# Two modulation groups moved into the loop over the first two units, their loads ahead of the residual's spill, and the reads of the gate tile shared by two engines

## What is computed

```python
mod = (jax.nn.silu(c) @ w_ada + b_ada)[:, None, :]
sh1, sc1, gt1, sh2, sc2, gt2 = jnp.split(mod, 6, axis=-1)
h = rmsnorm(x, g_mix) * (1 + sc1) + sh1
z = h @ w_in
u, q, k, v, o, ig, fg, gp, gm = jnp.split(z, IN_SPLITS, axis=-1)
# a pooling mixer on u, an mLSTM on q, k, v, ig, fg, merge gates gp, gm, then
x = x + gt1 * (merged @ w_out)
# and an FFN with its own modulation sh2, sc2, gt2, and a last norm
```

## Time and profile before

| | us |
|---|---|
| median of 3 executions | 1986.21 (1984.85 to 1988.93) |
| the profiled execution | 1987.68 |
| its span, first to last instruction | 1985.5 |
| PE busy | 1912.7 (96%) |
| DVE, ACT, POOL busy | 698.3, 450.1, 103.6 |
| mean granted clock of PE | 0.983 of 2.4 GHz |

### The profile page before, as it was taken

One profiled execution on the slowest core, in us unless ns is written; L12 is line 12 of the kernel. 1 busy time (PEld: TensorE's weight loads), 2 busy tenths in 40 slices (PEclk: granted clock), 3 DMA queues, 4 the chain that ended last, 5 costly groups with the idle time before them and its releaser, 6 DMA issues.

```text
span 1985.5 us, 28627 instructions
## 1 busy us (share of the span) xinstructions
PE 1912.7 (96%) x11797; PEld 1847.4 (93%) x11797; DVE 698.3 (35%) x1240; ACT 450.1 (23%) x708; POOL 103.6 (5%) x217
## 2 busy tenths in 40 slices
PE   7999999999999999887899999999999999999997
PEld 5899999999999999766799999999999999999997
DVE  5311110013333333343735482343343244244236
ACT  5321211123333333412202122111111111111113
POOL 0010047010000000021000000000000000000000
PEclk9999999999999999988899999999999999999999
DMA  9653345342333333587743401111111111111102
GB/s 338 224 166 127 122 138 158 120 140 70 103 102 102 102 102 102 152 223 248 254 147 101 142 12 64 43 43 42 42 42 53 42 42 42 42 42 50 45 32 90
DMA packets 219344, 211.12 MB, mean 106 GB/s; under 512 B 13499, under 2 KB 187439, under 8 KB 219279
## 3 DMA queue, kind: packets, MB, share of 16 engines
q1 hardware_dynamic: 210093, 176.29, 29.1%
q10 hardware_dynamic: 7786, 29.57, 3.7%
q0 software_dynamic: 1408, 4.46, 0.7%
HBM read 156.00 MB, written 54.41 MB: 106 GB/s over the span
## 4 chain that ended last, share of the span: by engine, by line
PE 90%; DMA 4%; DVE 3%; ACT 1%; SPq 1%; issue 1%; ACTq 0%; DVEq 0%
PE dense L1867 79%; PE misc L2116 1%; PE misc L2120 1%; DMA z_scratch<-stage 1%; PE dense L2293 1%; PE misc L1956 1%; PE misc L2089 1%; DMA out_dram<-cst 1%; PE misc L2118 1%; PE dense L1924 1%; DMA out_dram<-cs 1%; SPq L587 1%; PE misc L2227 0%; PE dense L2016 0%; PE misc L2097 0%
## 5 line engine op out<-in xcount | busy, mean ns | idle before, releaser
L1867 PE MATMUL dense<-act_hi,w_hi 128*128 128x384 f32 (+1 forms) x2616 | 615.8, 342 | 11.8 <-DVE act_lo L1288 6.8
L1867 PE MATMUL dense<-act_hi,w_lo 128*128 128x384 f32 (+1 forms) x2616 | 583.1, 329 | 0.0
L1867 PE MATMUL dense<-act_lo,w_hi 128*128 128x384 f32 (+1 forms) x2616 | 583.0, 329 | 0.0
L1867 PEld LDWEIGHTS dense<-act_hi,w_hi 128*128 128x128 f32 x2616 | 451.8, 189 | 28.8 <-issue 15.6
L1867 PEld LDWEIGHTS dense<-act_hi,w_lo 128*128 128x128 f32 x2616 | 450.0, 189 | 3.0 <-issue 3.0
L1867 PEld LDWEIGHTS dense<-act_lo,w_hi 128*128 128x128 f32 x2616 | 448.9, 189 | 1.3 <-issue 1.3
L1273 DVE TENSOR_TENSOR w_lo<-raw,w_hi 128x1024 fp32r<-128x1024 f32 x131 | 160.9, 1229 | 508.7 <-ACT w_hi L857 508.6
L857 ACT ACTIVATE w_hi<-raw 128x1024 fp32r<-128x1024 f32 x132 | 139.8, 1059 | 298.3 <-PE dense L1867 287.4
L1867 PE MATMUL dense<-a_hi,w_lo 128*128 128x384 f32 (+1 forms) x480 | 106.3, 329 | 0.0
L1803 DVE SCALAR_TENSOR_TENSOR hmT<-dense,mod,hmT 128x768 f32<-128x768 f32 x80 | 81.4, 1017 | 69.3 <-PE dense L1867 68.8
L1867 PE MATMUL dense<-a_lo,w_hi 128*128 128x384 f32 (+1 forms) x480 | 105.7, 328 | 0.0
(11 more groups left out here) (316 smaller groups left out, 1519.5 us busy)
## 6 DMA issues: line engine op xcount, KB each, us to landing
z_scratch<-stage ACTq DMA_DIRECT2D x52, 544.0 KB, 2.7
raw<-in_w_in_dram SPq DMA_DIRECT2D x53, 512.0 KB, 3.6
raw<-in_w_gate_up_dram SPq DMA_DIRECT2D x44, 512.0 KB, 3.6
ada_w<-in_w_ada_dram SPq DMA_DIRECT2D x20, 1024.0 KB, 7.0
stage<-z_scratch SPq DMA_DIRECT2D x24, 544.0 KB, 3.8
raw<-in_w_down_dram SPq DMA_DIRECT2D x22, 512.0 KB, 3.5
oin<-z_scratch SPq DMA_DIRECT2D x16, 544.0 KB, 4.4
qkv<-z_scratch SPq DMA_DIRECT2D x8, 1024.0 KB, 6.0
```

The lines of the kernel that those rows point to most:

```text
L1867: ins = pe.matmul(tile(k, c), w[:, off:off + P], x[:, xr, t0:t1], start=(first and p == 0), stop=(last and p == 2))
```

## The change

On SP, ada loads 8 and 9 go ahead of the spill of xT; 10 and 11 stay behind it. On PE, groups 8 and 9 are computed inside the loop: product 8 at the end of step kk = 4, turn 8 in step 5, product 9 at the end of step 5, turn 9 in step 6. ACT reads their rows and mods between the high parts of the last four row blocks. Once the gate tile is full, ACT makes the high split of weight tile 2 first and then reads only the gate rows of partitions 0 to 7; DVE copies those of partitions 32 to 39 and then makes the low split.

```diff
@@ SP
             for j in range(2):
                 load(2 + j, w_cols(w_in[0], P * (1 + j)))
+            for a in range(KT, ADA0 // 2):
+                ada_load(a)
 
             for s in range(2):
                 sp.wait_ge(tile_free[s], T_SS // 2)
             sp.dma_start(z[Z_X:Z_X + KT].rearrange("k p t -> p k t"), xT[:, :, :]).then_inc(x_spilled, 16)
 
-            for a in range(KT, ADA0 // 2 + 2):
+            for a in range(ADA0 // 2, ADA0 // 2 + 2):
                 ada_load(a)
@@ ACT
             for p in range(1, KT // 2):
-                if p < KT // 2 - 1:
-                    h_high(2 * p)
-                    group_mod(2 * p + 2)
-                    h_high(2 * p + 1)
-                    group_rows(2 * p + 3)
-                    group_mod(2 * p + 3)
-                    if 2 * p + 4 < KT:
-                        group_rows(2 * p + 4)
-                else:
-                    h_high(2 * p)
-                    h_high(2 * p + 1)
-            for a in range(KT, ADA0 // 2):
-                ada_out(a)
+                h_high(2 * p)
+                group_mod(2 * p + 2)
+                h_high(2 * p + 1)
+                group_rows(2 * p + 3)
+                group_mod(2 * p + 3)
+                if 2 * p + 4 < ADA0 // 2:
+                    group_rows(2 * p + 4)
             act.wait_ge(rest_in, rest)
 
             wait_full(act, tile_full, T_GATE)
+            split_hi(2)
             s = 3 * (T_GATE % 2)
-            for a in range(2):
-                kw_ = {"bias": gbias[:, 0:1]} if a == 0 else {}
-                rows, p0 = gates[32 * a:32 * a + 8, :], 32 * a
-                act.activation(wide(rows), dense[p0:p0 + 8, s:s + 2, 0:384], ACT.Copy if a else ACT.Identity, **kw_
-                               ).then_inc(gates_ready, 1)
-                act.activation(rows[:, 768:T], dense[p0:p0 + 8, s + 2, 0:320], ACT.Copy if a else ACT.Identity, **kw_
-                               ).then_inc(gates_ready, 1)
+            act.activation(wide(gates[0:8, :]), dense[0:8, s:s + 2, 0:384], ACT.Identity, bias=gbias[:, 0:1]
+                           ).then_inc(gates_ready, 1)
+            act.activation(gates[0:8, 768:T], dense[0:8, s + 2, 0:320], ACT.Identity, bias=gbias[:, 0:1]
+                           ).then_inc(gates_ready, 1)
             act.wait_ge(gates_ready, 4)
             act.sem_inc(tile_free[T_GATE % 2], 1)
-            split_hi(2)
@@ DVE
             for p in range(KT // 2):
                 first_rows(p)
+            wait_full(dve, tile_full, T_GATE)
+            s = 3 * (T_GATE % 2)
+            dve.tensor_copy(wide(gates[32:40, :]), dense[32:40, s:s + 2, 0:384]).then_inc(gates_ready, 1)
+            dve.tensor_copy(gates[32:40, 768:T], dense[32:40, s + 2, 0:320]).then_inc(gates_ready, 1)
             split_lo(2)
@@ PE
                     one_pass(T_L1, 1, P * kk, kk, p, kk == 0, end, act_hi, act_lo)
-                    if p == 0 and kk + 3 < KT:
+                    if p == 0 and kk + 3 < ADA0 // 2:
                         group_turn(kk + 3)
                 one_pass(T_L1, 1, P * kk, kk, 2, kk == 0, end, act_hi, act_lo)
-                if kk + 4 < KT:
+                if kk + 4 < ADA0 // 2:
                     group_product(kk + 4)
-            for a in range(KT, ADA0 // 2):
-                group_product(a)
-                group_turn(a)
```

## The result

The changed kernel took 1989.03 us at the median of 20 executions (1987.22 to 1995.16), the kernel before 1986.05 on the same chip (20 executions, 1982.23 to 1990.20). The ratio is 1.0016, 95% interval 1.0009 to 1.0022: slower by 1.8 to 4.4 us.

The account below looks back on a forecast made before the run. The prediction took L1867's dense matmuls as the bound, losing time in the gap ahead of unit 2 and at half clock. A start 0.5 us later less 0.25 gave about +0.3, median 1986.5 us, range 1983.0 to 1990.2.

Parts of the forecast that it names:

- What bounds the stage: Between loop and unit 2: a 9.7 us gap, then half clock costing unit 2 1.95 us; at most about 11.7 us.
- Part 1: Groups 8 and 9 inside the loop: products at 61.4 and 65.5 without waits, adding 3.24 us; 4.9 leave the gap.
- Part 2: Split first, gate reads shared by ACT and DVE: low split done at 73.8, unit 2 could start at 73.9.
- Part 3: Spill behind load 9 on SP: load 10 lands at 77.4, unit 2 starts at 79.1, 0.5 us later than before.
- The half clock: In unit 2: 3.4 us lie at half clock instead of 3.9, which gives 0.25 us back.
- The sum: Whole kernel: +0.5 for unit 2's start less 0.25 of half clock, about +0.3 us, median 1986.5.
- B: Ahead of unit 2: load 10 isn't held back, landing before 72.9; unit 2 at 73.9, full clock, 1979.6 us; chance 0.15.
- C: Idle ahead of group 10's product: clock doesn't fall, product takes 1.00, unit 2 at 78.5; -2.1 us, 1984.1; chance 0.10.
- D: Ahead of unit 2: load 10 at 80.6 beside ACT's store, unit 2 at 82.3, longer half clock; +5.1, 1991.3; chance 0.07.

Follow-up runs that it names:

- the first pair: First traces of the unchanged kernel before and of the changed kernel; unit 2 ends 1.6 us later in the changed one.
- the second: Second traces of the same two kernels, nothing altered in either; unit 2 ends 2.2 us later in the changed one.

## Why the prediction was right, and where its number was off

- **What bounds the stage.** Right: the gap ahead of unit 2 and the clock behind it. Both were to be had: unit 2 ends at 88.3 with the old order of loads and at 87.2 with load 10 ahead as well, against 92.6 before, all of it at full clock.
- **Part 1.** Right to the tenth: products at 61.75 and 65.89 (61.4 and 65.5, the whole start 0.4 us later), no wait, ACT's late row block unnoticed. The remark that loads 8 and 9 as slow as before (7.5 and 6.2) would cost 0.3 us was sound for the wait, 0.53 us with a load 8 of 7.65; but the load can take 9.0, and then it was 1.92 and 1.6 more at half clock.
- **Part 2.** Right: copies of 0.95 and 0.47 (0.96 and 0.4), low split done at 74.2 (73.8 and the 0.4 of the start).
- **Part 3.** Right in mechanism: the spill ahead of load 10 in one queue, a wait on ada_w, half clock behind it. The sizes: load 10 at 79.1 and not 77.4, made of the start (0.4), load 9's flight (6.3, not 5.4), the spill (11.1, not 10.7). The product took 1.94, not the 1.66 of a trace in which part of it ran at full clock. So unit 2 at 81.1 instead of 79.1. That load 10 left at 62.93, where I had 62.6, was luck: I held it back by 3.71 us for the spill's issue, which took 0.53, and what held it was its ring buffer, given back as group 8's rows were read at 62.9. The half clock gave 0.86 back in the first pair, 0.7 in the second, where I had 0.25: unit 2 started later than I had it, and lay in the stretch at half clock for 2.1 us (81.1 to 83.2) instead of 4.0 (78.6 to 82.6).
- **The sum.** +0.3 forecast; +1.6 and +2.2 at the end of unit 2 in the two pairs, +3.2 (1.8 to 4.4) at the medians. The mis-sized term is the landing of load 10, 1.3 us without the shift of the start. The 1.5 us near 275 stood in no term. That the median lies in the range owes something to its width, which holds the scatter of single executions.
- **The rivals.** B needed load 10 by 72.9: it took another order of issue. C fell, the clock was 0.59 at the mean from 75.8 to 79.1 and the product took 1.94. D had a landing of 80.6; load 10 landed midway between that and the forecast's 77.4, and +3.2 is nearer to D's +5.1 than to +0.3. The condition given for D, a landing later than 77.0, did not part it from the forecast, whose own landing is later too. D's reason failed: ACT's store, issued at 75.22, took 6.3 us instead of 2.8, but no packet of it moved before 79.1, when load 10 had landed, so it cost load 10 nothing. And where two queues do meet, the engines were not halved between them: the shares went by rows, so long rows beside a load would have taken four fifths.

The Trainium skill (DMA: Bandwidth & Descriptors, "Queues, rings and completion order") has the descriptors of a ring consumed in ring order: the landings of the changed kernel agree, 11.1 and 3.0 us apart. It also has the DMA engines change between queues at packet granularity: the pair with load 10 in ACT's queue agrees, 16.6 us beside long rows and 10.2 beside short ones, with 696 rows to 698 and 926 to 925. Whether the engines change after every row or after a run of rows, these counts don't tell.

## What to carry to other kernels

When loads are moved ahead of a large store, ask which transfer now stands first behind it, and when its consumer comes in the engine's order: here the two loads that were moved had 1.9 and 0.8 us to spare, and the third, left behind, held up all that followed for 6.6. One line further, with load 10 ahead as well, the change gave 4 to 9 us. Most of that is the work in the loop and the shared reads: with the loads left behind the spill it gave 3.6 to 8.4. Another queue was no way past a store with long rows, since the two queues' shares went by rows and not by bytes. And compare where the stage ends, not only where it starts: a later start met less half clock and gave part of the loss back.

## What was not expected of the hardware

- A 1 MB load of 1 KB rows, alone 5.2 to 5.4 us, takes 15.5 and 16.6 us beside a 4.46 MB store with 4352-byte rows in another queue, and ends with it; beside the same store in 1088-byte rows 10.2. The two queues move row for row (696 to 698, 926 to 925).
- A transfer issued while the other queue is at work can be long without a first packet: 3.6 and 3.8 us for load 10 in ACT's queue, 3.9 for the store of unit 1 (75.22 to 79.1), 1.0 for a load with nothing else under way.
- The issue of a transfer can hold the issuing engine long: three of 1088 KB each, behind a first one, took ACT's list 8.13 us, one of 4352 KB 0.43.
- The same 1.78 us pause cost PE either nothing or 1.5 us of half clock, six and eight times in fourteen traces, while an idle time of 3.05 us ahead of unit 2 cost none in one trace, and one of 1.92 us inside the loop 1.6 us in another.
